# Splitting the S5 gate, LRU and RWKV output matrices of a hybrid decoder into three-term products

## The reference

```python
z = x @ w_in[l]                                    # 1024 -> 6400 columns
y_s5  = (gelu(s5(z_s5)) @ glu_w1) * sigmoid(gelu(s5(z_s5)) @ glu_w2)
y_lru = (h * gelu(z_ly)) @ lru_w_out               # h: gated linear recurrence over a causal convolution
y_rw  = ((groupnorm(y) + bonus) * g) @ rw_w_out    # y: RWKV-7 delta-rule state over all positions
merged = g0 * y_s5 + g1 * y_lru + g2 * y_rw        # g: three sigmoid gates of 1024 channels
x = layer_norm(ALPHA * x + merged @ mix_w_out[l])
```

## Time and profile before

| | |
|---|---|
| median of the runs | 1746.96 us |
| profiled execution | 1747.89 us, span 1746.1 us |
| mean granted TensorE clock | 0.984 |
| PE busy | 1635.3 us |
| DVE busy | 1105.5 us |
| ACT busy | 756.7 us |
| POOL busy | 318.3 us |
| plain products (L718) | 512 records, 0.216 us from one to the next |

### The profile page before, as it was taken

The page is one execution under the profiler, slowest core; times in us unless marked ns, Lnnn a source line. Parts: engine busy times, 40 slices in busy tenths (PEclk is TensorE's granted clock), DMA queues, the critical chain, the costliest instruction groups (busy, mean ns, idle before and its releaser), DMA issues.

```text
span 1746.1 us, 32946 instructions
## 1 busy us (share of the span) xinstructions
PE 1635.3 (94%) x14300; PEld 1508.1 (86%) x14300; DVE 1105.5 (63%) x1394; ACT 756.7 (43%) x978; POOL 318.3 (18%) x205
## 2 busy tenths in 40 slices
PE   6999979999989998999989999899999999989996
PEld 6889979988889887999989898898888888879995
DVE  3576579757546666544476756897474567584445
ACT  3454443553243444444455445345332434444442
POOL 1124440000000133210150435200000004050102
PEclk8999999999999999999999999999999999999998
DMA  6765645433345545566676565453334355456663
GB/s 188 187 182 174 195 115 146 133 115 92 96 124 174 167 130 148 180 185 188 206 178 182 172 181 168 132 157 111 96 96 125 108 190 152 141 148 186 187 182 120
DMA packets 380616, 267.84 MB, mean 153 GB/s; under 512 B 21084, under 2 KB 361400, under 8 KB 380472
## 3 DMA queue, kind: packets, MB, share of 16 engines
q1 hardware_dynamic: 377624, 255.25, 50.2%
q10 hardware_dynamic: 2848, 10.49, 1.7%
HBM read 264.66 MB, written 1.05 MB: 152 GB/s over the span
## 4 chain that ended last, share of the span: by engine, by line
PE 72%; DVE 18%; ACT 4%; POOL 2%; issue 2%; DMA 1%; SPq 0%; DVEq 0%; ACTq 0%; POOLq 0%
PE bank L705 14%; PE bank L706 13%; PE bank L707 13%; PE banks4to L707 6%; PE banks4to L706 6%; PE banks4to L705 6%; DVE ring_lo L1671 5%; PE bank L718 5%; ACT ring_hi L1284 1%; ACT work L1284 1%; DVE small L1690 1%; DVE x_tok L1685 1%; PE banks4to L1075 1%; DVE xT_lo L1718 1%; PE bank L1239 1%
## 5 line engine op out<-in xcount | busy, mean ns | idle before, releaser
L1671 DVE TENSOR_TENSOR ring_lo<-ring_raw,ring_hi 128x1024 fp32r<-128x1024 f32 x438 | 591.0, 1354 | 403.8 <-ACT ring_hi L1284 391.1
L1284 ACT ACTIVATE ring_hi<-ring_raw 128x1024 fp32r<-128x1024 f32 x444 | 468.3, 1057 | 532.2 <-PE bank L707 317.4
L705 PE MATMUL bank<-xT_hi,ring_hi 128*128 128x256 f32 x2224 | 639.5, 288 | 26.8 <-DVE ring_lo L1671 16.9
L706 PE MATMUL bank<-xT_lo,ring_hi 128*128 128x256 f32 x2224 | 631.6, 284 | 0.0
L707 PE MATMUL bank<-xT_hi,ring_lo 128*128 128x256 f32 x2224 | 631.4, 284 | 0.0
L705 PEld LDWEIGHTS bank<-xT_hi,ring_hi 128*128 128x128 f32 x2224 | 428.9, 193 | 40.1 <-issue 28.7
L706 PEld LDWEIGHTS bank<-xT_lo,ring_hi 128*128 128x128 f32 x2224 | 428.9, 193 | 1.6
L707 PEld LDWEIGHTS bank<-xT_hi,ring_lo 128*128 128x128 f32 x2224 | 428.9, 193 | 0.0
L2255 POOL TENSOR_TENSOR hT_lo<-work,hT_hi 128x512 fp32r<-128x512 f32 x44 | 78.7, 1789 | 512.2 <-ACT hT_hi L1284 511.9
L707 PE MATMUL banks4to<-ring_hi,hT_lo 128*128 128x512 f32 x352 | 140.6, 399 | 0.0
L706 PE MATMUL banks4to<-ring_lo,hT_hi 128*128 128x512 f32 x352 | 140.4, 399 | 0.0
(11 more groups left out here) (310 smaller groups left out, 2152.0 us busy)
## 6 DMA issues: line engine op xcount, KB each, us to landing
ring_raw<-in_w_in_dram SPq DMA_DIRECT2D x100, 512.0 KB, 3.9
ring_raw<-in_ffn_wg_dram SPq DMA_DIRECT2D x88, 512.0 KB, 3.9
ring_raw<-in_ffn_wu_dram SPq DMA_DIRECT2D x88, 512.0 KB, 3.8
ring_raw<-in_ffn_wd_dram SPq DMA_DIRECT2D x88, 512.0 KB, 3.5
ring_raw<-in_xa_wkv_dram SPq DMA_DIRECT2D x32, 512.0 KB, 4.0
ring_raw<-in_s_glu_w_dram SPq DMA_DIRECT2D x16, 512.0 KB, 3.4
ring_raw<-in_mix_w_out_dram SPq DMA_DIRECT2D x16, 512.0 KB, 3.5
ring_raw<-in_xa_wq_dram SPq DMA_DIRECT2D x16, 512.0 KB, 3.9
```

Source lines behind the costliest of these rows:

```text
L705: mm(o, a[0], b[0], start=first, stop=False, **kw)
L706: mm(o, a[0], b[1], start=False, stop=False, **kw)
L1284: return nc.scalar.activation(o, i, func, **kw)
L1671: st.mark(tt(lo_flat(n), raw_flat(n), hi_flat(i), ALU.subtract), s_lo["dve"])
```

## The change

All pieces are now split. `PLAIN` becomes `SQUARE` and only names the shape. ScalarE makes the high halves of the 16 new pieces a layer and of three activations (`zu`, `ly`, `wk[0]`); POOL makes the low halves of the 12 pieces of w1, w2 and lru and of `zu` and `ly`, VectorE those of rw's four pieces and of `wk[0]`. PE waits for the low half of the activation ahead of the first product and for each piece's low half. The low half of gate 8's two pieces moves on VectorE from the solver's fourth step to behind its fifth and behind the first state copy. Two views in `region_z` move by a few columns.

```diff
-PLAIN = ("w1", "w2", "lru", "rw")
-POOL_LO = [("g0", 0, 0), ("g1", 0, 0), ("z", 0, 0)]
+SQUARE = ("w1", "w2", "lru", "rw")
+POOL_LO = [(k, j, m) for k in ("w1", "w2", "lru") for j in range(2) for m in range(2)]
+POOL_LO += [("g0", 0, 0), ("g1", 0, 0), ("z", 0, 0)]
...
-        LX_AT = 1024 + RWT * (T + 1)
+        LX_AT = 1024 + RWT * (T + 1) + 2
...
+        zu_r = [rounded("zu_hi", z_at, 2048, NW, T), rounded("zu_lo", z_at, 0, NW, T)]
+        ly_r = [rounded("ly_hi", z_at, LX_AT, NW, T), rounded("ly_lo", z_at, LY_AT, NW, T)]
+        yc_r = [rounded("yc_hi", w_at, 9216, NW, T), rounded("yc_lo", w_at, 4096, NW, T)]
...  half_chunk, on PE
-                    n = number(kind, j, m)
-                    loaded(pe, n)
-                    w, o = slot(raw, n % RAW, NW, 256), claim(kind, j, m)
+                    w, o = take(kind, j, m), claim(kind, j, m)
...
-                            last = mm(o[:, c * T:(c + 1) * T], w[:, k, c * P:(c + 1) * P], src[:, k, :],
-                                      start=(k == 0), stop=(k == NW - 1))
+                            last = mm3(o[:, c * T:(c + 1) * T], [x[:, k, c * P:(c + 1) * P] for x in w],
+                                       [x[:, k, :] for x in src], k == 0, k == NW - 1)
...  PE, ahead of w1
-                pe.wait_ge(*at(s_ys5, NW))
-                by_channel("w1", 0, zu)
+                pe.wait_ge(*at(s_zul, 1))
+                by_channel("w1", 0, zu_r)
...  PE, solver, ahead of solve_Y
                     if i == 3:
-                        pe.wait_ge(*at(s_yl, NW))
+                        pe.wait_ge(*at(s_lyl, 1))
...  PE
-                pe.wait_ge(*at(s_yrw, 1))
-                by_channel("rw", 0, wk[0])
+                pe.wait_ge(*at(s_ycl, 1))
+                by_channel("rw", 0, yc_r)
...  ScalarE
                 gate_evac(2)
+                act.wait_ge(*at(s_ops, 1))
+                act.wait_ge(*at(s_ys5, NW))
+                st.mark(f(zu_r[0], zu, ACT.Copy), s_zuh)
+                hi_to("w1", 0, further=False)
                 gate_evac(3)
...  behind the first pair of token copies, the second, glu_sigmoid(0), the LRU gates, the exponentials
+                hi_to("w2", 0, further=False)
+                hi_to("w1", 1, 0, further=False)
+                hi_to("w1", 1, further=False)
+                hi_to("w2", 1, 0, further=False)
+                hi_to("w2", 1, further=False)
...  in the solver's steps; before, step 3 had hi_to("gate", 8)
+                    if i == 2:
+                        act.wait_ge(*at(s_yl, NW))
+                        st.mark(f(ly_r[0], ly, ACT.Copy), s_lyh)
+                        hi_to("lru", 0, 0, further=False)
+                    if i == 3:
+                        hi_to("lru", 1, 0, further=False)
...
                 hi_to("v", 0)
+                act.wait_ge(*at(s_yrw, 1))
+                st.mark(f(yc_r[0], wk[0], ACT.Copy), s_ych)
                 v_evac(0)
+                hi_to("rw", 0, further=False)
...  VectorE
                         st.mark(v.tensor_copy(X_[:, 0::2, :], bank(6, 8, C)), s_Vd)
+                        lo_to("gate", 8, 0, further=False)
                         for k in range(4, 8):
                             merge(k)
...
-                    if i == 3:
-                        lo_to("gate", 8, further=False)
...
+                lo_to("v", 0, further=False)
+                dve.wait_ge(*at(s_ych, 1))
+                st.mark(tt(yc_r[1], wk[0], yc_r[0], ALU.subtract), s_ycl)
                 lo_to("v", 1, 0)
...  POOL
+                pool.wait_ge(*at(s_zuh, 1))
+                st.then(tt(zu_r[1], zu, zu_r[0], ALU.subtract), s_zul)
+                for j in range(2):
+                    for k in ("w1", "w2"):
+                        piece_lo(k, j, 0)
+                        piece_lo(k, j, 1)
                 pool.wait_ge(*at(s_Nb, 4))
                 st.then(tt(M_, M_, const("eye2").unsqueeze(1).to_broadcast([P, NQ, C]), ALU.add), s_Me)
+                pool.wait_ge(*at(s_lyh, 1))
+                st.then(tt(ly_r[1], ly, ly_r[0], ALU.subtract), s_lyl)
+                for j in range(2):
+                    piece_lo("lru", j, 0)
+                    piece_lo("lru", j, 1)
```

More of the change, by code:

```diff
@@ L154 @@
 for _n, _x in enumerate(PIECES * L):
[L155 to L158, removed]
+    _who = "pool" if _x in POOL_LO else "dve"
+    SPLIT_AT[_n] = len(SPLIT_AT)
+    LO_AT[_n] = (_who, sum(w == _who for w, _ in LO_AT.values()))
 SPLITS = list(SPLIT_AT)
@@ L202, in trunk @@
         reg_r, r_at = sb("region_r", 8192)
-        reg_z, _ = sb("region_z", 4 * T + RWT * (T + 1) + 4 * (T + 3) + 4 * T + 6)
+        reg_z, z_at = sb("region_z", 4 * T + RWT * (T + 1) + 4 * (T + 3) + 4 * T + 6)
         work, w_at = sb("work", 10240)
@@ L267, in trunk @@
         V_AT = 1024 + 8 * (T + 1)
-        LX_AT = 1024 + RWT * (T + 1)
+        LX_AT = 1024 + RWT * (T + 1) + 2
         lx = view(reg_z, LX_AT, NW, T + 3)
-        ly = view(reg_z, LX_AT + NW * (T + 3), NW, T)
+        LY_AT = LX_AT + NW * (T + 3) + 4
+        ly = view(reg_z, LY_AT, NW, T)
         memtok = view(reg_z, LX_AT, 2, D)
+        zu_r = [rounded("zu_hi", z_at, 2048, NW, T), rounded("zu_lo", z_at, 0, NW, T)]
+        ly_r = [rounded("ly_hi", z_at, LX_AT, NW, T), rounded("ly_lo", z_at, LY_AT, NW, T)]
+        yc_r = [rounded("yc_hi", w_at, 9216, NW, T), rounded("yc_lo", w_at, 4096, NW, T)]
         b_raw = [view(reg_z, 256 * i, NS, 16) for i in range(2)]
@@ L417, in trunk @@
         s_ys5 = sem("s5_gelu", 4)
+        s_zuh, s_zul = sem("s5_gelu_hi", 1), sem("s5_gelu_lo", 1)
+        s_lyh, s_lyl = sem("lru_y_hi", 1), sem("lru_y_lo", 1)
+        s_ych, s_ycl = sem("rwkv_gated_hi", 1), sem("rwkv_gated_lo", 1)
         s_conv = sem("lru_conv", 4)
@@ L539, in rows @@
                 return part.rearrange("(k p) n -> p k n", p=P), nk, n
-            if kind in PLAIN:
+            if kind in SQUARE:
                 w = {"w1": "s5_glu_w1", "w2": "s5_glu_w2", "lru": "lru_w_out", "rw": "rw_w_out"}[kind]
@@ L995, in _ @@
                 last.then_inc(s_tok, 1)
-                by_channel("w2", 0, zu)
+                by_channel("w2", 0, zu_r)
                 pe.wait_ge(*at(s_toke, 4))
@@ L1004, in _ @@
                     last.then_inc(s_lg, 1)
-                half_chunk("w1", 1, 0, zu)
+                half_chunk("w1", 1, 0, zu_r)
                 for g in range(4):
@@ L1010, in _ @@
                     if g == 2:
-                        half_chunk("w1", 1, 1, zu)
+                        half_chunk("w1", 1, 1, zu_r)
                     if g >= 2:
@@ L1029, in _ @@
                 last.then_inc(s_N, 1)
-                half_chunk("w2", 1, 0, zu)
+                half_chunk("w2", 1, 0, zu_r)
                 for par in range(2):
@@ L1039, in _ @@
                     last.then_inc(s_N, 1)
-                half_chunk("w2", 1, 1, zu)
+                half_chunk("w2", 1, 1, zu_r)
                 for par in range(2):
@@ L1048, in _ @@
                 gate(4)
-                fill = [("gate", 5, xT), ("gate", 6, xT), ("gate", 7, xT), ("lru", 0, ly), ("lru", 1, ly)]
+                fill = [("gate", 5, xT), ("gate", 6, xT), ("gate", 7, xT), ("lru", 0, ly_r), ("lru", 1, ly_r)]
                 ORDER = ((0, 0), (1, 1), (0, 1), (1, 0))
@@ L1202, in _ @@
                 memory_values(0)
-                pe.wait_ge(*at(s_yrw, 1))
-                by_channel("rw", 0, wk[0])
-                by_channel("rw", 1, wk[0])
+                pe.wait_ge(*at(s_ycl, 1))
+                by_channel("rw", 0, yc_r)
+                by_channel("rw", 1, yc_r)
                 memory_values(1)
@@ L1481, in _ @@
                     st.mark(f(SV[C:P, :, 2 * b:2 * b + 2, :], bank(4 + b, 4, 2, C)[C:P], ACT.Copy), s_toke)
+                hi_to("w1", 1, 0, further=False)
                 glu_sigmoid(0)
-                hi_to("gate", 4, 0)
+                hi_to("w1", 1, further=False)
                 for g in range(2):
@@ L1494, in _ @@
                     st.mark(f(a_[:, t, :], a_[:, t, :], ACT.Exp, scale=sp8n[:, t:t + 1]), s_lga)
+                hi_to("w2", 1, further=False)
                 act.wait_ge(*at(s_lq, 1))
                 st.mark(f(th_, th_, ACT.Sqrt), s_lm)
+                hi_to("gate", 4, 0)
                 glu_sigmoid(1)
@@ L1504, in _ @@
                     if i == 3:
-                        hi_to("gate", 8)
+                        hi_to("lru", 0, further=False)
                     if i == 4:
+                        hi_to("lru", 1, further=False)
                         act.wait_ge(*at(s_V, 17))
                         st.mark(f(X_[:, 1::2, :], bank(7, 8, C), ACT.Copy), s_Va)
+                        hi_to("gate", 8, 0, further=False)
                         break
```

## The result

The kernel after takes 1774.15 us (median of four runs, 1772.68 to 1775.48) against 1747.10 (1746.74 to 1747.63) for the one before in the same session: a ratio of 1.0155, 95% interval 1.0139 to 1.0172, **27.05 us slower**. The forecast was 17 us slower, 1764, and its range ended at 1771: the direction was right, the size too small.

The account below looks back on a forecast made before the run. The prediction took TensorE, busy 94% of the span, as the bound. Its terms, 2.4 (w1/w2), 5.5 (lru) and 0.6 (rw), summed to 8.5 us a layer, 17.0 for both: 1764 us, range 1752 to 1771.

Parts of the forecast that it names:

- What the products give back: Three-term half chunks in w1, w2, lru, rw: 0.61 us saved each, 19.5 us in all if nothing waits.
- w1's start: At w1's first product, PE waits for GpSimd's low halves and starts 1.9 us late.
- The lock between VectorE and GpSimd: In w1/w2, GpSimd subtractions hold up VectorE's convolution steps; PE waits 3.5 us at the transposes.
- Rival 2: In w1/w2, short VectorE steps are not locked out: -1.2 instead of +2.4 a layer, 1756.8 us; chance 0.23 with similar errors.
- The lru chain: Late ly copy and low halves: PE waits about 3.2 and 1.4 us at solver and first half, some 4 at state product.
- rw: In the rw stretch, later pieces outweigh shorter products: +0.6 us a layer, between -2.4 and +2.
- rival 3: GpSimd's subtractions take 3.20 instead of 2.40 us throughout: 3.2 us a layer more, 1770.4 us; chance 0.13.
- the sum behind each wait: After the small products' wait, full-rate product times are added up to gate 4: start at 419.4 instead of 417.04.
- w1/w2: Stretch up to gate 4: 2.4 us later a layer in spite of 4.9 us saved.
- lru with gate 8: Stretch from lru through gate 8's state product: +5.5 us a layer, between +2.2 and +7.1.

Follow-up runs that it names:

- best2: best1 with GpSimd waiting for VectorE's token copies and w2's last piece moved to VectorE: 1739.24 us, ratio 0.9950 to the kernel before.
- only_lru: The change with the LRU matrix alone split, gate 8's low halves moved with it; w1, w2 and rw plain: 1761.72 us, ratio 1.0085 to before.
- only_rw: The change with the RWKV matrix alone split; w1, w2 and lru plain: 1747.01 us, ratio 1.0000 to before.
- act_delay: The kernel before with throwaway ScalarE copies ahead of its share of the token copies, so PE waits at the second transposes: 1757.82 us (single run).
- best1: Kernel after with GELU(y), first w1 and w2 chunks' low halves on VectorE, ly rounded earlier, gate 8's low halves on GpSimd: 1750.37 us.

## Why the prediction was right in direction and too small

- *What the products give back: right.* A half chunk falls from 3.66 to about 3.04 us; with its waits and slow stretches mostly removed, best2 shows 7.8 of the 19.5 us as net gain.
- *w1's start: right.* 1.82 us of wait against 1.9 forecast (the prediction's own times, 369.6 against 367.85, give 1.75).
- *The lock between VectorE and GpSimd: right.* The short convolution steps are held up, about one GpSimd subtraction each: 5.51 us for three, 1.84 each, where the sum had 2.5; but the tensor-scalar step between them, which the sum let through, took 2.38. The wait is 3.73 at the transposes (3.5 forecast). For the small products the prediction gives a start 3.5 us later than before (404.75); it is 5.3 later, behind a wait of 4.43, and 1.4 of the difference are the slow transposes. Rival 2 falls. The Trainium skill, SBUF — State Buffer (Who interferes with whom), says that a VectorE instruction with two SBUF inputs contends with a GpSimd instruction that reads SBUF. The trace agrees for steps of 256 elements too.
- *The lru chain: its waits right, all but one.* 3.04 us against 3.2 ahead of the solver's product. The second is 0.47 against 1.4, because that product ran 0.9 us longer at the lower clock and filled it. The one ahead of the state product was named at some 4 us and is 2.12, with 0.59 and 0.58 one product before and behind it; the prediction's own times give about 3 for it.
- *rw: right.* 0.5 against 0.6 a layer, and alone too little to see.
- *GpSimd at 3.20 (rival 3): wrong.* The 30 subtractions take 2.43 us in the mean.
- **The step that failed** is the sum behind each wait, "From there: 1.1 + half 3.05 + products 3.75 + half 3.05 + 3.7", and its like in the lru part. It counts what follows a wait at full rate. The terms were 2.4 (w1/w2) and 5.5 (lru with gate 8); they measured 5.6 and 8.4 in the first layer, and the 5.95 us of products at the lower clock there are the whole difference. In the second they measured 4.6 and 5.6, and the rw term 2.1 for 0.6, with 3.5 us net of slow products. The prediction read the one slow stretch of before, put it at 1.7 us, and did not ask what preceded it: a wait of 2 us. The change made three new waits of 2 to 4 us a layer in those two terms (3.73, 3.04, 2.12), lengthened one of 2.0 to 4.4, and added one of 1.8 at w1.

The Trainium skill, TensorE: Matmul & The Clock Gate (Why this matters for your kernels), says that idle gaps between bursts of matmuls lower PE's clock. The traces here agree behind the waits of 3.0 to 4.4 us (clock 0.50 to 0.76 in the windows shown). Behind waits of 1.8 to 2.3 us it fell in some executions and layers, and in others not.

**What stays open.** What decides whether a wait of about 2 us costs clock: the same wait of 2.0 us, with the same work around it, is harmless in the first layer of before and not in the second. No run varied it alone. Over the kept traces the wait of 2.0 us ahead of the small products was followed by slow products in 4 of 8 cases (before, only_lru, only_rw, act_delay, two layers each), and that of 1.8 us ahead of the last half of `mix` in 12 of 22 (all eleven kernels; in both layers of best2, in neither of before). So some of the slow halves above may come and go with the execution; each kernel has only one trace. The second layer of best1 adds one more harmless case (2.16 us ahead of its gate products, which then take 3.34 us to the next product, as in best2), its first layer one that cost 1.7 us (1.86 us of wait). The gain of best2 over best1 is accounted for only roughly: the profiled spans differ by 15.0 us (1748.7 and 1733.7); the waits that are gone make 8.1 of them and the slow products 5.6. The medians differ by 11.1 only; the profiled execution of best2 was one of its two fastest.

## What to carry to other kernels

Price a wait of TensorE at its length plus the slow stretch behind it: here 1.4 to 2.8 us more behind each of the 22 waits of 3.0 to 4.4 us that the traces have in this stage (of which 0.9 can hide behind a second wait), and 1.4 to 1.8 us or nothing behind waits of 1.8 to 2.4 us. When work is handed to GpSimd "because it is idle", look for the VectorE instructions with two SBUF tensors that run beside it, and who waits for the last of them: each short one can be held up for a whole GpSimd subtraction (0.4 to 0.5 us becomes 1.8 to 2.4). Where such a chain is late by little, hold GpSimd back until VectorE has delivered: best2 won 11 us over best1 by one more wait and one piece moved. The two steps were not run apart.

## What the runs showed of the hardware that was not expected

- Filling TensorE's waits with products that nobody reads made the kernel 8.4 us faster (1765.7 against 1774.2 us), with the granted clock at 1.00 where it had been 0.50 to 0.63.
- The largest wait is not the only one that costs clock: the last half of `mix`, behind a wait of 1.78 to 1.81 us, took 4.48 us instead of 2.97 in the second layer of the kernel after (clock 0.63) and 2.98 in its first (clock 1.00).
- A VectorE tensor-scalar step (line 1930) with a single tensor in SBUF, beside its per-partition columns, was held up by GpSimd as well: 2.38 us at 368.99, 0.41 at 362.99, before GpSimd began. The Trainium skill, SBUF — State Buffer (Who interferes with whom), counts `tensor_scalar` among the operations that can enter a mode that uses both port pairs, and would then be held up; the row agrees.
- GpSimd hardly suffers when VectorE's steps are short: its four subtractions in a row took 9.96 us, 2.49 each, against 3.3 beside steps of 1024 elements.
